# Two transformer-style layers on one core: the router's logits turned whole with the mean square as a column, two modulation chunks moved among the second layer's input projections, and the last output piece split at another point of ScalarE's order

## The chip, the cores and the metric

The kernel runs on one core of a Trainium2 chip. Time is the device time of one execution in microseconds (us). A core has TensorE (PE; PEld is its weight load), VectorE (DVE), ScalarE (ACT), GpSimd (POOL) and SyncE (SP), each with its own instruction stream, and 16 DMA engines that all queues share. Engines wait for one another by semaphores. TensorE's clock is granted at one of two levels, 1.2 or 2.4 GHz; the profile gives it as a share of 2.4.

## The reference, cut to what matters

Two layers over 128 context tokens and 512 latent tokens of width 1024, all in fp32. Each layer has mixers between an input and an output projection, then an expert-choice mixture of 16 experts (capacity 64 latent and 16 context tokens each). Six modulation vectors per layer and group come from a 1024 x 6144 product.

```python
for layer in range(DEPTH):
    sh1, sc1, g1, sh2, sc2, g2 = modulation(c, w_mod[layer], b_mod[layer])   # silu(c) @ w_mod + b_mod, in six
    h = rms_norm(x, norm1[layer]) * (1 + sc1) + sh1
    x = x + g1 * mixers(h)                       # input projections, attention and gating or conv, output projection
    h = rms_norm(x, norm2[layer]) * (1 + sc2) + sh2
    x = x + g2 * ec_moe(h, moe_router[layer], ...)
# ec_moe: aff = softmax(h @ w_router); gate, idx = top_k(aff, cap) for each expert; SwiGLU of the gathered rows
```

## The kernel before

**Layout.** The residual x is kept turned (`xT`: features on 128 partitions, 8 feature tiles of 640 tokens). A weight piece is 128 x 2048 elements (1 MB). It is loaded by SyncE into a place, split by ScalarE into a high part `w_hi` (`split`, L1582, L1593, L1886) and by VectorE into the rest `w_lo` (L1998, L1996), and multiplied by TensorE in three passes (`passes`, `project`, `project_by_rows`). There are four stage slots that go round in the order of the stream (`staged()` in `plan_weights`), some lent places in other buffers, and three split slots. A load waits for the last user of its slot: for a split piece until its low part is made (`lo_ready`), for a modulation half until TensorE has used it (`mod_used`, or the chunk's rows being full). SyncE issues the loads strictly in the order of the stream (L732), so a wait holds up all behind it.

**Modulation chunks.** 24 chunks of 512 columns (12 a layer), each two 1 MB halves that are not split. `mod_rows(c)` on TensorE makes the rows (16 matmuls on 32-column groups), ScalarE copies them from PSUM to `mrow`, `turn_mod(c)` turns them by four transposes, VectorE reduces and adds the bias (L2072, L2075). `MOD_AT` says where each chunk stands in the order; `mod_before` and `mod_place` follow from it. The two chunks of `"next norm"`, 16 and 17 (the gate of layer 1's mixers, used at its output projection), stand between layer 1's first norm and its first input projection `cq`.

**Orders written out by hand.** PSUM has 8 banks. `plan_psum` lists every use of a bank in TensorE's order and who empties it; `begin`, `filled` and `emptied` wait by that list. The four engine programs (`block.tensor`, `block.scalar`, `block.vector`, `block.gpsimd`) repeat the same order, each for its own part, so that an engine that waits holds up what stands behind it.

**Output projection (both layers).** Eight tiles m, two to a weight piece `(L, "out", j)`. VectorE adds each into x (L2322) and from m = 3 on makes `h_sum` = x times scale (L2340). Beneath the tiles TensorE does the chunks of `MOD_AT[(L, "out")]` (rows after an even m, turn after the next m). ScalarE splits piece 3, then goes through `squares_for_pool` (L1595): for each m it squares x (L1604), copies chunk rows (L1580), and after m = 0 the turned shift, which goes to DRAM. GpSimd adds the squares of tiles 0 to 6 (L812).

**Ranking.** The router's logits are made in four column groups of TensorE, each summing two feature tiles, as two halves of 320 tokens; squares summed over features come as one column per token tile (`token_sums`, weights = the squares, moving = one column of 1/1024). ScalarE copies the logits, TensorE turns them and adds the four groups at once by a product with `fold` (five token tiles, 16 columns each). VectorE and ScalarE make the root (L2344, L1625, L1628, L2347 to L2349), the softmax (L2358 to L2366). TensorE turns three row tiles of h, then the affinities (L1421), then two more row tiles, the rows of the chunks of `(L, "rank")` and, in layer 1, x. ScalarE scales and copies the row tiles, GpSimd adds the shift (L886), SyncE stores them (L780). VectorE picks the top 64 and 16 in rounds of eight (L2373 to L2376); after the second round it converts the context's indices (L2379, a cast) and adds 512 (L2380), at the end it converts the others (L2381). Then come the gates, the slots (L2393), the gathers (L895, which wait for all row stores and for the slots) and the experts.

**Start of layer 1.** When the experts' sum is read back (`acc_in`), TensorE turns it, VectorE adds it into x, ScalarE squares (L1684), TensorE sums, VectorE makes the variance (L2017), its part of the split of `cq`, and the root's Newton step. SyncE waits for `acc_in` before the first half of chunk 16. GpSimd waits for the second half of chunk 17 before its small loads. The input projections then run `cq`, `ckv`, `gc`, `hv`, `gb`, two pieces each of the last three.

## Time and profile before

| | |
|---|---|
| three timed runs | 1398.42 us median (1397.84 to 1402.41) |
| the profiled execution | 1397.08 us, span 1395.3 us, mean granted clock 0.947 |
| TensorE busy | 1272.9 us, 91% of the span |
| VectorE busy | 870.8 us, 62% |
| ScalarE busy | 707.4 us, 51% |
| GpSimd busy | 242.9 us, 17% |
| chain that ended last | TensorE 76%, DMA 10%, ScalarE 7%, VectorE 6% |

How to read it. The profile is of one execution; times in it are us from the start of the span. A line of the timeline gives start, length, engine, source line, operation, written and read tensors, shape and count, and in brackets how long the engine had been idle before it and what released it. TensorE's matmuls are pipelined and their ends are modelled; an fp32 matmul shows as two records. The layer-0 mixers run from 39 to 340 us, its ranking to 384, its experts to 674; layer 1 follows: input projections 711 to 831, attention to 964, output projections to 1034, ranking to 1076, experts to the end.

### The profile page before, as it was taken

The page shows a single profiled execution, that of the slowest core. Times are in us where ns is not written, and L with a number is a line of the kernel's source. Part 1 is how long each engine was busy: PE and PEld are TensorE (multiplying, and loading weights), DVE is VectorE, ACT ScalarE, POOL GpSimd, SP SyncE. Part 2 cuts the span into 40 slices and gives each one's busy share as a digit, 9 for nine tenths or more (in the row PEclk, how much of TensorE's full clock was granted, in tenths as well). Part 3 has the DMA queues.
Part 4 walks back from the last instruction along what each step waited for, and adds up shares of the span by engine and source line. Part 5 has one row for each costly group of instructions (what it writes and reads, how often), then busy time and mean ns, then how long its engine had stood idle before and what let it go on. Part 6 is the DMA issues. An engine that isn't in the chain of part 4 may idle for free.

```text
span 1395.3 us, 18223 instructions
## 1 busy us (share of the span) xinstructions
PE 1272.9 (91%) x7584; PEld 923.8 (66%) x7584; DVE 870.8 (62%) x1007; ACT 707.4 (51%) x821; POOL 242.9 (17%) x135
## 2 busy tenths in 40 slices
PE   5999988999399999999789998999994999999997
PEld 2887856788266666666469984667892666666562
DVE  5613556422678888888475252553226799999894
ACT  3531147511467777777343123554115677776772
POOL 3100000011502222211030000000124033333330
PEclk9997899999699999999989999899997999999997
DMA  9810182042799999999893221002409999999984
GB/s 358 248 63 31 39 290 82 1 151 91 285 350 350 385 380 380 384 392 396 289 267 103 91 82 57 1 1 91 151 31 356 372 381 378 385 387 382 398 295 160
DMA packets 100471, 324.98 MB, mean 233 GB/s; under 512 B 6719, under 2 KB 30494, under 8 KB 84006
## 3 DMA queue, kind: packets, MB, share of 16 engines
q1 hardware_dynamic: 89376, 290.88, 55.5%
q0 software_dynamic: 8400, 27.58, 7.8%
q10 hardware_dynamic: 2614, 5.35, 1.1%
q8 instruction: 60, 0.98, 0.3%
q14 instruction: 21, 0.17, 0.0%
HBM read 300.29 MB, written 23.50 MB: 232 GB/s over the span
## 4 chain that ended last, share of the span: by engine, by line
PE 76%; DMA 10%; ACT 7%; DVE 6%; issue 1%; SPq 0%; ACTq 0%
PE psum L939 71%; ACT arena L1812 3%; DMA stage<-in_w_mod 3%; DVE arena L2264 2%; DMA arena<-in_moe_w_up 2%; DMA h_hi<-h_dram,arena 2%; DVE w_lo L1996 1%; PE psum L1463 1%; DMA stage<-in_moe_w_gate 1%; ACT arena L1580 1%; DMA arena<-in_od_w_in 1%; ACT w_hi L1886 1%; PE psum L1412 1%; PE psum L1497 1%; PE psum L1016 1%
## 5 line engine op out<-in xcount | busy, mean ns | idle before, releaser
L939 PE MATMUL psum<-w_hi,h_hi 128*80 128x512 f32 (+1 forms) x848 | 330.6, 390 | 9.9 <-DVE w_lo L1996 6.5
L1996 DVE TENSOR_TENSOR w_lo<-stage,w_hi 128x2048 fp32r<-128x2048 f32 (+1 forms) x122 | 275.5, 2270 | 94.5 <-ACT w_hi L1593 56.4
L939 PE MATMUL psum<-w_lo,h_hi 128*80 128x512 f32 (+1 forms) x848 | 325.8, 384 | 0.0
L939 PE MATMUL psum<-w_hi,h_lo 128*80 128x512 f32 (+1 forms) x848 | 325.1, 383 | 0.0
L1886 ACT ACTIVATE w_hi<-stage 128x2048 fp32r<-128x2048 f32 x100 | 190.5, 1915 | 56.8 <-PE psum L939 37.0
L939 PE MATMUL psum<-h_hi,w_hi 128*128 128x320 f32 x672 | 214.3, 319 | 1.4 <-DVE h_lo L2043 1.4
L939 PE MATMUL psum<-h_hi,w_lo 128*128 128x320 f32 x672 | 211.5, 315 | 0.0
L939 PE MATMUL psum<-h_lo,w_hi 128*128 128x320 f32 x672 | 211.3, 315 | 0.0
L904 POOL DMA_INDIRECT acc_dram<-arena x31 | 120.2, 3879 | 411.0 <-ACT arena L1918 227.0
L1996 DVE TENSOR_TENSOR w_lo<-arena,w_hi 128x2048 fp32r<-128x2048 f32 x73 | 166.7, 2288 | 35.7 <-ACT w_hi L1886 31.8
L939 PEld LDWEIGHTS psum<-w_hi,h_hi 128*80 128x80 f32 (+1 forms) x848 | 129.9, 153 | 84.1 <-issue 14.0
L939 PEld LDWEIGHTS psum<-w_hi,h_lo 128*80 128x80 f32 (+1 forms) x848 | 129.9, 153 | 63.8 <-issue 1.6
L939 PE MATMUL psum<-arena 128*64 128x128 f32 (+7 forms) x964 | 147.3, 398 | 20.1 <-ACT arena L1812 9.9
L939 PEld LDWEIGHTS psum<-w_lo,h_hi 128*80 128x80 f32 (+1 forms) x848 | 130.2, 154 | 52.9 <-issue 1.2
L1886 ACT ACTIVATE w_hi<-arena 128x2048 fp32r<-128x2048 f32 x71 | 134.9, 1913 | 20.2 <-PE psum L939 16.1
L939 PEld LDWEIGHTS psum<-arena 128*64 128x64 f32 (+4 forms) x964 | 83.3, 177 | 86.9 <-issue 61.5
L939 PEld LDWEIGHTS psum<-h_hi,w_hi 128*128 128x128 f32 x672 | 129.9, 193 | 6.4 <-issue 6.2
L939 PEld LDWEIGHTS psum<-h_lo,w_hi 128*128 128x128 f32 x672 | 129.6, 193 | 0.2 <-issue 0.2
L939 PEld LDWEIGHTS psum<-h_hi,w_lo 128*128 128x128 f32 x672 | 129.3, 192 | 0.0
L1580 ACT ACTIVATE arena<-psum 128x512 f32<-128x512 f32 (+7 forms) x125 | 65.0, 576 | 99.3 <-PE psum L939 82.0
L1812 ACT ACTIVATE arena<-psum,arena 128x640 f32<-128x640 f32 x64 | 50.2, 789 | 63.5 <-DVE arena L2264 63.5
L2322 DVE SCALAR_TENSOR_TENSOR xT<-psum,mod,xT 128x320 f32<-128x320 f32 (+2 forms) x48 | 18.1, 433 | 100.0 <-PE psum L939 100.0
(267 smaller groups left out, 1315.1 us busy)
## 6 DMA issues: line engine op xcount, KB each, us to landing
stage<-in_w_mod SPq DMA_DIRECT2D x46, 1024.0 KB, 7.7
stage<-in_moe_w_up SPq DMA_DIRECT2D x36, 1024.0 KB, 15.7
stage<-in_moe_w_down SPq DMA_DIRECT2D x34, 1024.0 KB, 14.5
stage<-in_moe_w_gate SPq DMA_DIRECT2D x30, 1024.0 KB, 14.5
arena<-in_moe_w_gate SPq DMA_DIRECT2D x29, 1024.0 KB, 16.5
arena<-in_moe_w_up SPq DMA_DIRECT2D x23, 1024.0 KB, 15.2
arena<-in_moe_w_down SPq DMA_DIRECT2D x19, 1024.0 KB, 15.2
xT<-in_moe_w_down SPq DMA_DIRECT2D x11, 1024.0 KB, 20.6
```

Of the source, the lines that this page charges most:

```text
L904: pool.indirect_dma_start(acc_dram[L], bass.IndirectOffsetOnAxis(slots[:, e:e + 1], 0), ysb[e % 2], None, compute_op=ALU.add).then_inc(sca ...
L939: return pe.matmul(o, w, x, start=first, stop=last, skip_group_check=True)
L1016: ins = pe.transpose(bank(("mod turned", c))[:, P * b:P * b + P], mrow[:, P * b:P * b + P], ident)
L1412: ins = pe.transpose(pair((L, "h", t), n=D)[:, P * k:P * k + P], h_sum[k][:, P * t:P * t + P], ident)
L1463: ins = pe.transpose(psum[:, k // 4, CAP * (k % 4):CAP * (k % 4) + CAP], xs[s][:, P * k:P * k + P], ident[0:CAP, 0:CAP])
L1497: ins = pe.transpose(psum[:, 2, CAP * f:CAP * f + CAP], hid[:, P * f:P * f + P], ident[0:CAP, 0:CAP])
L1580: freeing(nc.scalar.activation(dst, src, ACT.Copy, **kw))
L1812: ins = nc.scalar.activation(p[:, LKEYS * a:LKEYS * a + LKEYS], src[:, 0:LKEYS], ACT.Exp, bias=largest(i, a), accum_out=total(i, a))
L1886: nc.scalar.activation(split_slot(w_hi, pc["q"]), slot(pc), ACT.Copy).then_inc(hi_ready, 1)
L1996: return nc.vector.tensor_tensor(dst, src, hi.bitcast(F32), ALU.subtract)
L2264: ins = nc.vector.tensor_reduce(largest(i, a), src[:, 0:LKEYS], AX.X, ALU.max, negate=True)
L2322: ins = nc.vector.scalar_tensor_tensor(xT[:, m, tk], src, mod[:, L, 2, m, g:g + 1], xT[:, m, tk], ALU.mult, ALU.add)
```

## The change

- Chunks 16 and 17 leave the start of layer 1. Chunk 16 stands after the second `gc` piece, chunk 17 after the second `hv` piece, in the weight stream and on all engines. SyncE waits for `acc_in` before `cq`, GpSimd for `cq`.
- The logits are made for 512 latent and 128 context tokens, in two banks. A matrix `mean_` (zeros, column 16 = 1/1024) is multiplied with the sum of squares in column group 0 and with the last square in group 1, so that row 16 of the groups holds the mean square. ScalarE copies the latent part, VectorE the context part, five transposes turn all, and VectorE adds the four groups by one reduction of 17 columns for five token tiles. The root is made from column 16, after the turn.
- Two row tiles, not three, are turned ahead of the affinities.
- ScalarE splits output piece 3 after the square of m = 1, inside `squares_for_pool`, instead of ahead of it.
- The two index conversions become one instruction each, max(index, index + 512) and max(index, index + 0), written as fp32.

```diff
-          "acc": [13, 14, 15], "next norm": [16, 17], "cq": [18, 19], ...
+          "acc": [13, 14, 15], "gc": [16], "hv": [17], "cq": [18, 19], ...
...
@@ plan_weights: the stream
-            chunk(MOD_AT["next norm"][0])
...
-            if kind == "cq":
-                chunk(MOD_AT["next norm"][1])
+            if (kind, m) in (("gc", 1), ("hv", 1)):
+                mod(kind)
...
@@ SyncE, GpSimd
-                    if L > 0 and pc["key"] == ("mod", MOD_AT["next norm"][0], 0):
+                    if L > 0 and pc["key"] == in_keys(L)[0]:
...
-                    pc = piece[("mod", MOD_AT["next norm"][1], 1)]
+                    pc = piece[in_keys(L)[0]]
...
@@ TensorE
-                    mod_rows(MOD_AT["next norm"][0])
-                    turn_mod(MOD_AT["next norm"][0])
-                    mod_rows(MOD_AT["next norm"][1])
...
-                    turn_mod(MOD_AT["next norm"][1])
...
                     project(("gc", 1), [("gc", 2), ("gc", 3)])
+                    modulation("gc")
                     for kind in ("hv", "gb"):
                         for j in range(2):
                             project((kind, j), [(kind, 2 * j), (kind, 2 * j + 1)])
+                        if kind == "hv":
+                            modulation("hv")
                     modulation("cq")
...
+                def column_group(g, weights, moving, tk, first, last):
+                    o = bank((L, "logits")) if tk is LAT else bank((L, "logits ctx"))[:, 0:NC]
+                    return mm(o[32 * g:32 * g + 32, :], weights, moving[:, tk], first, last)
+
+                for tiles in ((0, 1, 2, 3), (4, 5, 6)):
                     pe.wait_ge(x_scaled, KD * L + tiles[-1] + 1)
+                    for tk in GROUPS:
                         for k in tiles:
+                            column_group(k % 4, router[:, L, k, :], h_sum[k], tk, k < 4, k >= 4)
...
+                pe.wait_ge(mean_ones, 1)
                 pe.wait_ge(sq_added, added[0])
+                pe.wait_ge(x_scaled, KD * (L + 1))
                 pe.wait_ge(sq_ready, squared[0])
+                for tk in GROUPS:
+                    column_group(3, router[:, L, KD - 1, :], h_sum[KD - 1], tk, False, True)
+                    column_group(0, mean_[:, :], rstd, tk, False, True)
+                    column_group(1, mean_[:, :], sq[(KD - 1) % 2], tk, False, True).then_inc(psum_full, 1)
                 name = (L, "logits turned")
+                emptied(pe, (L, "logits ctx"))
+                emptied(pe, (L, "logits"))
                 begin(name)
                 for t in range(NT):
-                    at = E * TILE_AT[t]
-                    ins = mm(bank(name)[:, at:at + E], lgT[:, P * t:P * t + P], fold[:, :], t == 0, t == NT - 1)
+                    at = P * TILE_AT[t]
+                    ins = pe.transpose(pair(name)[:, at:at + P], lgT[:, P * t:P * t + P], ident)
...
-                for t in range(3):
+                for t in range(2):
                     turn_tile(t)
                 pe.wait_ge(aff_done, L + 1)
...
+                turn_tile(2)
                 turn_tile(3)
...
@@ ScalarE, squares_for_pool
                     if k % 2 == 0 and k // 2 < len(under):
                         modulation((L, "out"), slice(k // 2, k // 2 + 1))
+                    if which == 1 and k == 1:
+                        split((L, "out", 3))
...
@@ ScalarE, layer 1's projections
                     for m in (2, 3):
                         evacuate(("gc", m), two(zT[:, m, :]), halves(("gc", m)))
+                    modulation("gc")
                     split(keys[6])
                     split(keys[7])
                     split((L, "out", 0))
+                    modulation("hv")
                     split((L, "out", 1))
...
-                split((L, "out", 3))
                 squares_for_pool(L, 1, (L, "T", len(STEPS) - 1, 2))
-                evacuate((L, "logits"), two(lgT), halves((L, "logits")))
-                root_of(L, 1)
+                evacuate((L, "logits"), lgT[:, LAT], bank((L, "logits")))
+                act.wait_ge(token_var_ready, L + 1)
+                nc.scalar.activation(token_root, token_var, ACT.Ln).then_inc(log_done, 1)
...
@@ VectorE
+            then(nc.vector.memset(mean_[:, :], 0.0))
+            nc.vector.tensor_copy(mean_[:, E:E + 1], ones_d[:, 0:1]).then_inc(mean_ones, 1)
...
                     split(keys[5])
+                    modulation("gc")
                     split(keys[6])
...
                     split((L, "out", 0))
+                    modulation("hv")
...
+                freeing(nc.vector.tensor_copy(lgT[:, CTX], bank((L, "logits ctx"))[:, 0:NC]))
+                name = (L, "logits turned")
+                filled(dve, name)
+                parts = pair(name).rearrange("p (t g r) -> p t r g", t=NT, g=4)[:, :, 0:E + 1, :]
+                freeing(nc.vector.tensor_reduce(token_sums, parts, AX.X, ALU.add))
+                emptied(dve, name)
+                column = token_var.rearrange("p (t o) -> p t o", o=1)
+                nc.vector.tensor_scalar(column, token_sums[:, :, E:E + 1], EPS, None, ALU.add).then_inc(token_var_ready, 1)
...
-                        ctx_idx = idxf[CTX_ROW:RANKED, 0:CAP_C]
-                        then(nc.vector.tensor_copy(ctx_idx, idx[CTX_ROW:RANKED, 0:CAP_C]))
-                        nc.vector.tensor_scalar(ctx_idx, ctx_idx, float(NL), None, ALU.add).then_inc(ranked_ctx, 1)
-                nc.vector.tensor_copy(idxf[0:2 * E, :], idx[0:2 * E, :]).then_inc(topk_done, 1)
+                        found = idx[CTX_ROW:RANKED, 0:CAP_C]
+                        nc.vector.scalar_tensor_tensor(idxf[CTX_ROW:RANKED, 0:CAP_C], found, float(NL), found, ALU.add, ALU.max).then_inc(ranked_ctx, 1)
+                found = idx[0:2 * E, :]
+                nc.vector.scalar_tensor_tensor(idxf[0:2 * E, :], found, 0.0, found, ALU.add, ALU.max).then_inc(topk_done, 1)
```

## Rows read from the trace of the kernel before

**Rows 1.** The page: the span.
```profile
span 1395.3 us, 18223 instructions
```

**Rows 2.** The chain of waits (start, length, what it went through).
```profile
690.94 10.19 DMA arena<-in_od_w_in
...
741.76 89.20 PE psum L939 x598
```

**Rows 3.** The timeline of the output projections, layer 0 (first two) and layer 1.
```profile
290.49 0.42 PEld L1016 LDWEIGHTS psum<-cst,mrow 128*128 128x128 f32 x4 [3.64 <-ACT small L1580]
...
299.65 0.16 PEld L939 LDWEIGHTS psum<-stage,sP 128*32 128x32 f32 x8 [0.19 <-issue]
...
981.96 1.13 DVE L2322 SCALAR_TENSOR_TENSOR xT<-psum,mod,xT 128x320 f32<-128x320 f32 x3 [9.01 <-PE psum L939]
982.02 1.91 ACT L1593 ACTIVATE w_hi<-stage 128x2048 fp32r<-128x2048 f32 x1 [16.82 <-PE psum L939]
983.84 0.72 ACT L1604 ACTIVATE arena<-xT 128x640 f32<-128x640 f32 x1
...
985.30 0.71 PEld L1016 LDWEIGHTS psum<-cst,mrow 128*128 128x128 f32 x4 [3.64 <-ACT small L1580]
...
986.28 1.74 SPq L732 DMA_DIRECT2D stage<-in_w_mod  x3
...
995.53 1.92 PE L939 MATMUL psum<-stage,sP 128*32 128x512 f32 x16
```

**Rows 4.** Busy by stretch: us, PE, PEld, DVE, ACT, POOL, clock, DMA share, GB/s.
```profile
984.00:986.00 2.00, 0.67 (x3) 0.70 (x4) 2.00 (x1) 1.19 (x3) 0.00 (x0) 0.56 0.00 0
```

**Rows 5.** DMA issues, 291.4 to 291.7 us (count, size, us to landing).
```profile
stage<-in_w_mod SPq DMA_DIRECT2D x1, 1024.0 KB, 5.1
```

**Rows 6.** The timeline of the ranking, layer 0 (first two) and layer 1.
```profile
340.37 2.35 PE L939 MATMUL psum<-arena,router 128*32 128x320 f32 x28
...
353.26 0.38 PE L1421 MATMUL psum<-cst,arena 128*32 128x128 f32 x2
...
1034.10 2.35 PE L939 MATMUL psum<-arena,router 128*32 128x320 f32 x28
...
1037.59 1.26 PE L939 MATMUL psum<-arena,router 128*32 128x320 f32 x4
...
1040.17 0.17 DVE L2344 TENSOR_SCALAR stat<-psum 128x5 f32<-128x5 f32 x1 [3.87 <-PE psum L939]
...
1041.52 0.24 DVE L2358 TENSOR_TENSOR arena<-psum,stat 128x80 f32<-128x80 f32 x1
...
1043.41 0.24 DVE L2366 TENSOR_TENSOR arena<-arena 128x80 f32<-128x80 f32 x1
...
1045.03 0.64 PE L1421 MATMUL psum<-cst,arena 128*32 128x128 f32 x2
```

**Rows 7.** Groups of VectorE's instructions by shape (busy us, mean ns).
```profile
L2264 DVE TENSOR_REDUCE arena<-psum 128x1 f32<-128x640 f32 x64 | 49.7, 819 | 30.3 <-PE psum L939 30.3
```

**Rows 8.** The timeline behind the affinities, layer 0.
```profile
356.85 9.29 POOL L886 TENSOR_TENSOR arena<-arena,h_hi 128x1024 f32<-128x1024 f32 x4 [2.70 <-ACT arena L1580]
...
359.26 2.29 DVE L2380 TENSOR_SCALAR arena<-arena 16x16 f32<-16x16 f32 x1
...
372.37 0.80 SPq L774 DMA_DIRECT2D arena<-in_moe_w_gate  x2
```

**Rows 9.** The timeline at the start of layer 1.
```profile
693.12 2.77 ACT L1684 ACTIVATE arena<-xT 128x640 f32<-128x640 f32 x4 [0.95 <-DVE xT L2062]
...
698.96 0.82 DVE L2017 TENSOR_SCALAR arena<-psum 128x640 f32<-128x640 f32 x1 [1.44 <-PE psum L939]
...
701.15 1.91 ACT L1593 ACTIVATE w_hi<-arena 128x2048 fp32r<-128x2048 f32 x1 [5.25 <-DMA arena<-in_od_w_in]
...
703.09 2.29 DVE L1996 TENSOR_TENSOR w_lo<-arena,w_hi 128x2048 fp32r<-128x2048 f32 x1 [3.31 <-ACT w_hi L1593]
```

**Rows 10.** The timeline of the ranking in layer 1: the turn of a chunk.
```profile
1054.63 0.42 PEld L1016 LDWEIGHTS psum<-cst,mrow 128*128 128x128 f32 x4 [1.68 <-ACT mrow L1580]
```

More of the change, by code:

```diff
@@ L105 @@
 MOD_AT = {"start": [2, 3, 0, 1], "qk": [4, 5], "first scores": [6, 7], (0, "out"): [8, 9, 10], (0, "rank"): [11, 12],
-          "acc": [13, 14, 15], "next norm": [16, 17], "cq": [18, 19], (1, "out"): [20, 21], (1, "rank"): [22, 23]}
+          "acc": [13, 14, 15], "gc": [16], "hv": [17], "cq": [18, 19], (1, "out"): [20, 21], (1, "rank"): [22, 23]}
 def mod_before(c):
@@ L195, in plan_psum @@
             one((L, "norm", 0), "dve", 2)
-            chunk, later_chunk = MOD_AT["next norm"]
-            one(("mod rows", chunk), "act"), one(("mod turned", chunk), "dve", in_order=False), one(("mod rows", later_chunk), "act")
         if L == 0:
@@ L225, in plan_psum @@
             one(("cq", 0), "act", 2), one(("cq", 1), "act", 2)
-            one(("mod turned", later_chunk), "dve", in_order=False)
-            for c in MOD_AT["next norm"]:
-                p.frees(("mod turned", c))
             one("ckv", "act", 2), one("kr", "act", 2)
@@ L235, in plan_psum @@
             one(("gc", 2), "act", 2), one(("gc", 3), "act", 2)
-            for kind in ("hv", "gb"):
-                for m in range(4):
-                    one((kind, m), "dve", 2)
+            mod("gc")
+            for m in range(4):
+                one(("hv", m), "dve", 2)
+            mod("hv")
+            for m in range(4):
+                one(("gb", m), "dve", 2)
             mod("cq")
@@ L434, in trunk @@
         router_ = sb("router", LAYERS * KD * 32)
-        fold = sb("fold", E)
+        fold, mean_ = sb("fold", E), sb("mean", 32)
         cst = sb("cst", C_USED)
@@ L1376, in logits @@
                     pe.wait_ge(x_scaled, KD * L + tiles[-1] + 1)
-                    for half in range(2):
-                        tk = slice(HT * half, HT * half + HT)
+                    for tk in GROUPS:
                         for k in tiles:
-                            g = 32 * (k % 4)
-                            ins = mm(bank((L, "logits"), half)[g:g + 32, 0:HT], router[:, L, k, :], h_sum[k][:, tk], k < 4, k >= 4)
-                    return ins
-                def token_sums(squares, first):
-                    for t in range(NT):
-                        at = TILE_AT[t]
-                        ins = mm(bank((L, "norm", 1))[:, at:at + 1], squares[:, P * t:P * t + P], ones_d[:, 0:1], first and t == 0, not first)
-                    return ins
@@ L1413, in turn_tile @@
                     ins.then_inc(psum_full, 1)
-                for t in range(3):
+                for t in range(2):
                     turn_tile(t)
@@ L1619, in squares_for_pool, with root_of @@
                                  bank((L, "shift logits"))[:, 0:2].rearrange("p (g o) -> p g o", o=1).to_broadcast([P, 2, P]))
-            def root_of(L, which):
-                emptied(act, (L, "norm", which))
-                squared, root = (var, rstd) if which == 0 else (token_var, token_root)
-                nc.scalar.activation(root, squared, ACT.Ln).then_inc(log_done, 1)
+            def root_of(L):
+                emptied(act, (L, "norm", 0))
+                nc.scalar.activation(rstd, var, ACT.Ln).then_inc(log_done, 1)
                 logs[0] += 1
                 act.wait_ge(log_done, logs[0])
-                nc.scalar.activation(root, root, ACT.Exp, scale=-0.5).then_inc(root_done, 1)
+                nc.scalar.activation(rstd, rstd, ACT.Exp, scale=-0.5).then_inc(root_done, 1)
             def shifted(L):
@@ L1639, in shifted @@
                         modulation("start", slice(3, None))
-                    if L > 0 and k == 3:
-                        modulation("next norm", slice(1, 2))
             def modulation(at, part=slice(None)):
@@ L1673, in _ @@
             split(in_keys(0)[0])
-            root_of(0, 0)
+            root_of(0)
             modulation("start", slice(2, 3))
@@ L1678, in _ @@
                 if L > 0:
-                    filled(act, (L - 1, "norm", 1))
+                    filled(act, (L - 1, "logits ctx"))
                     for k in range(KD):
@@ L1686, in _ @@
                     split(keys[0])
-                    root_of(L, 0)
-                    modulation("next norm", slice(0, 1))
+                    root_of(L)
                 shifted(L)
@@ L2126, in _ @@
                 split(keys[1])
-                if L > 0:
-                    modulation("next norm")
                 split(keys[2])
```

40 lines of the change are left out of this document (17 added, 23 removed).

## The prediction, on record before the changed kernel was seen

> **What bounds the kernel now.** I read the page first. The profiled execution has a span of 1395.3 us [rows 1] and 1397.08 us in all, so 1.8 us lie around the span; the three timed runs have their median at 1398.42, 1.3 above it. Then the chain of waits: TensorE carries three quarters of it, with stretches such as 89.2 us of back-to-back projections in the second layer [rows 2]. So work moved onto TensorE inside such a stretch costs its whole length, and what matters elsewhere is each place at which TensorE waits. I went to four of them with the timeline: the output projections of both layers, the ranking between projections and experts, the start of layer 1, and the layer-1 projections into which the two chunks move.
>
> **Output projections (the split of output piece 3 moved on ScalarE).** The edit is small in the diff, but the timeline shows a stall there. At the end of output tile 1 ScalarE first splits piece 3 (982.02, 1.91 us), then squares x (0.72), and only then copies the chunk rows for which TensorE waits; TensorE idles 3.64 us and turns the chunk at 985.30 [rows 3]. Layer 0 has the same 3.64 us, ending at 290.49 [rows 3]. The granted clock falls with it, to a mean of 0.56 of 2.4 GHz, so it is at 1.2 GHz for most of that stretch [rows 4], and output tile 2, 48 matmuls that take 7.1 us at the pace of [rows 2] (89.2 / 598 = 0.149 each), takes 8.8 in layer 0 (to 299.65) and 9.5 in layer 1 (986.0 to 995.53) [rows 3]. With the change the square and the copies of tile 0 come first and TensorE turns its chunk at once. That would give back 5.1 and 5.8 us. But something is late next. The split of piece 3 now stands behind the update of x (1.13) and the square (0.72), so the low half is done about 1.8 us later, and its slot is what the second half of the next chunk is loaded into: SyncE issues that load at 986.28 now [rows 3], and would at 988.1. It lands 5.1 us later [rows 5], at 993.2, while TensorE wants it at 982.5 + 7.1 + 1.0 = 990.6. The chunk's rows (1.92 us, half behind the load) end at 994.1 in place of 997.4: a gain of 3.3. In layer 0 by the same sum the load is issued at 293.3, lands at 298.4, and the rows end at 299.4 in place of 301.6: 2.2. Each now has an idle of 2.8 us, somewhat shorter than the 3.64 after which the clock fell; if it falls again, 1.7 to 2.4 go. I take 0.8 off each: **-1.4 and -2.5**. Ends: -0.5 and -0.9; and -5.1 and -5.8 if nothing is late.
>
> **Ranking.** Both layers do the same from the first group of router matmuls, G (1034.10 and 340.37) [rows 6]. Now: 2.35 us of them, ten one-column matmuls, the last router tile (1.26), ten more, then the turn by the fold. The root starts at G + 6.07 (L2344), the affinities' first step at G + 7.42 (L2358); they are ready at 1043.65, but TensorE is in the third tile and turns them 1.4 us later, at G + 10.93; in layer 0, where the clock is low, at G + 12.89 [rows 6]. After: 2.35, then the last tile and the two sets of mean columns in three different column groups side by side, as the first 14 matmuls are now (2.35 for what would be 8.8 alone), so 1.26; a copy of 512 columns by ScalarE (0.6, as the 0.58 to 0.72 of its neighbours), five transposes (0.8), a reduction of 340 elements, which I put at 0.5 between the 0.24 of 80 elements [rows 6] and the 0.82 of 640 [rows 7], and an addition. That makes the root start at G + 5.5, L2358 at G + 6.8, the affinities ready at G + 8.95 and turned at G + 9.1, as only two tiles stand ahead. Gain 3.8 in layer 0 and 1.8 in layer 1.
>
> What it is worth is read behind it. GpSimd's shifts start after ScalarE's second row tile and run 9.29 us without a gap; the last store of the rows lands just before 372.37, when SyncE goes on to the next weights, and the gather waits for the same [rows 8]. All of that moves with the affinities. The merged index instructions take 4.1 us out of the ranking on VectorE (L2379 and L2380 wait for GpSimd's shifts; the second takes 2.29 for 16 columns [rows 8]). I cost them at nothing: the store's landing covers the chain, which is done at about the same time now and would be early by this. If the new form waits for one shift, that is at most 2.3 back, still beneath the stores. In layer 1 the gate turn also waits for ScalarE's copies of x, which move by the 1.8. Against the gain: the DMA engines are full from the first expert pieces on, and those go out when TensorE has used chunk rows that now stand behind the third tile, so they move by 1.4 less, 2.4 and 0.4. I take the middle, **-3.1 and -1.1**.
>
> Here SyncE's loads of weights and GpSimd's gathers meet. The Trainium skill (DMA: Bandwidth & Descriptors, section Queues, rings and completion order) says that each DMA engine takes turns between the queues that have work. By that rule the gather wouldn't wait out SyncE's backlog, and the term would be the full 3.8 and 1.8, the sum 1.4 lower. No row here shows the turns themselves.
>
> **Start of layer 1.** The first projection's weights are issued third, behind the two halves of the removed chunk, and land 10.19 us later, at 701.1; ScalarE splits them (701.15), VectorE forms the low half (703.09, 2.29), and only then come the root, the scaled tiles and the first matmul [rows 2, 9]. Put first, they land after 5.1 [rows 5], at 695.1. That two loads ahead cost 5.1 together shows that one queue serves them in order. ScalarE is then in its squares until 695.9 and splits by 697.9; VectorE is held by the norm (698.96, 0.82 [rows 9]) and makes the low half at 699.8 in place of 703.09. **-3.3**; 1.0 if the load should take 10.2 after all. The removed chunk work costs nothing there today (TensorE idle) and its removal gives nothing. GpSimd's small loads start earlier, which nobody waits for.
>
> **The two chunks.** Both go into the 89.2 us stretch, without cover. Chunk 16, after the second gc piece: rows 1.92, then TensorE waits for ScalarE's copy, as at 1054.63 where it turns the rows after 1.68 of idle on the weight side, 0.8 after their end, and 0.5 for the turn [rows 3, 10]: **+3.1**. Its loads and its ring neighbours are early.
>
> Chunk 17, after hv, has another wait. Stage slots go round in fours. In the new order the pieces behind the first one are ckv, gc0, gc1, 16a, 16b, hv0, hv1, 17a, 17b, gb0, gb1, out0: out0 has the slot of 17a. So SyncE can't issue out0 until TensorE has used 17a. ScalarE, in its order, splits out0 and only then copies the rows of chunk 17, and TensorE stands before the turn for that copy. From the start of the rows: 0.96 (first half), 5.1 for the load, 1.95 for the split, 0.65 for the copy, 0.6 for the turn: 9.3 us. The idle of 7 us in it is longer than the one that lowered the clock in [rows 3, 4], so I add 1.8 for the restart: **+11.1** (9.3 to 11.8). VectorE's conv work behind its own split of out0 fits under the gb tiles.
>
> Before, the turn of chunk 17 stood after cq in a gap. Sum: -1.4 - 2.5 - 3.1 - 1.1 - 3.3 + 3.1 + 11.1 = **+2.8**. Against the profiled execution 1397.08 + 2.8 = 1399.9; with the median's 1.3 above it, **1401.2 us**. With every own term at its ends the sum goes from -1.5 to +10, that is 1397 to 1408.
>
> **Rivals.**
> - A: the forecast, chance 0.50.
> - B, slower: the clock. After each of the three idles (two of 2.8 us, one of 7) TensorE stays at 1.2 GHz longer, as after 985.30, where tile 2 lost 2.4 us. It decides if the 2.8 us idles already lower it. Price 1.6 at each output stage, 1.5 more at chunk 17, and the ranking, which begins colder, gives 1 less: about +5.5, 1406.7. For it: the fall at 3.64 in both layers, and ranking at low clock in layer 0 only. Chance 0.22.
> - C, faster: the wait at chunk 17 isn't there, because the slots fall otherwise than I count or the load is issued earlier. The 11.1 becomes 3.1, the sum -5.2: 1393.2. For it: only that I counted a ring. Chance 0.10.
> - D, faster: the loads at the output stages are in time, and all of 5.1 and 5.8 comes back: -7.0 more, 1394.2. Against it is the moved split itself. Chance 0.10.
> - E: the change does almost nothing, 1398.4, because the gains at the ranking end in a full DMA queue and the chunks hide in something that I don't see. Chance 0.08.
>
> **How the numbers follow.** 0.3% is 4.2 us, about what a measurement of this kernel tells from no change: slower begins at 1402.6, faster ends at 1394.2. A lies with a third of its chance above 1402.6 (0.16), B wholly (0.22): slower 0.38. Faster: most of C and half of D, 0.14. The rest, 0.48, is within. The range 1395 to 1407 takes in A, B and E with half of D, and leaves out C and the upper end of A.
>
> **What would show it.** In the profile after: TensorE turns chunks 8 and 20 with no idle before it; an idle of about 3 us inside the rows of chunks 9 and 21, released by a load; the first matmul of layer 1 at about 3 us sooner after the norm; after hv one idle of about 7 us ahead of a turn, with a load of in_od_w_out and its split in it; the index instructions gone from 4.1 us to 0.3 to 2.4; the gather no earlier than the row stores. Wrong would be the forecast if the idle after hv is under 3 us, or if the clock stays low for over 5 us after one of the three idles.

## The result, and the profile after

| | median of the runs | ratio to the kernel before, 95% interval |
|---|---|---|
| first comparison, 8 runs each | 1403.30 us (before: 1395.17) | 1.0068 [1.0045, 1.0090] |
| the same kernel again (`after_again`), 12 runs against 35 | 1399.42 us (before: 1394.82) | 1.0034 [1.0012, 1.0057] |

The changed kernel is slower by 0.3 to 0.7%, some 5 to 9 us. Both intervals lie above 1, and they overlap. The forecast was +2.8 us, 1401.2. The kernel before, at 1398.42 in the three runs known then, has its median near 1395 in the longer series, so the forecast is measured by its difference.

The profiled execution of the changed kernel took 1398.48 us, the shortest of its eight. It hides part of the loss, so I read a second one beside it. The page's busy line after; TensorE was 91% busy before:

```profile
span 1396.3 us, 18165 instructions
...
PE 1262.2 (90%) x7550; PEld 913.4 (65%) x7550; DVE 868.8 (62%) x1011; ACT 708.1 (51%) x821; POOL 235.6 (17%) x135
```

The chain of waits gives the borders of the stages. First further rows of the kernel before, for comparison with [rows 2] (start, length, what):

```profile
268.44 11.42 PE psum L939 x104
...
373.11 10.81 DMA h_hi<-h_dram,arena
...
680.62 5.98 DMA arena<-acc_dram
...
836.72 19.86 PE psum L939 x68
...
962.22 2.36 PE psum L939 x40
...
1065.80 10.58 DMA h_hi<-h_dram,arena
```

The same of the changed kernel:

```profile
268.78 11.43 PE psum L938 x104
...
293.55 5.21 DMA stage<-in_w_mod
...
370.59 8.85 DMA h_hi<-h_dram,arena
...
677.79 6.23 DMA arena<-acc_dram
...
801.62 5.34 DMA stage<-in_od_w_out
...
846.31 19.86 PE psum L938 x68
...
970.45 11.43 PE psum L938 x104
...
1069.51 8.24 DMA h_hi<-h_dram,arena
```

A stage is the distance between two of these: output projections and ranking from the x104 (or x40) row to the landing of the gather, experts to the landing of `acc_dram`, and so on. `copy_first`, `split_after_shift` and `best` are experiments told below. Each column is one execution.

| stage, us | before | after | after_again | copy_first | split_after_shift | best | forecast of the change |
|---|---|---|---|---|---|---|---|
| up to output projections, layer 0 | 268.4 | 268.8 | 269.8 | 271.4 | 270.8 | 268.9 | 0 |
| output projections and ranking, layer 0 | 115.5 | 110.7 | 109.5 | 109.7 | 108.2 | 108.3 | -4.5 |
| experts, layer 0 | 302.7 | 304.6 | 303.7 | 303.9 | 302.7 | 302.5 | 0 |
| start of layer 1 and its projections | 150.1 | 162.3 | 162.4 | 153.2 | 154.0 | 150.6 | +10.9 |
| attention, layer 1 | 125.5 | 124.1 | 124.2 | 123.2 | 123.2 | 123.2 | 0 |
| output projections and ranking, layer 1 | 114.2 | 107.3 | 111.1 | 109.8 | 109.5 | 110.2 | -3.6 |
| the rest | 318.9 | 318.6 | 318.8 | 317.9 | 318.7 | 317.6 | 0 |

One row carries the loss: +12.2 and +12.3 us where the chunks went in. It stands against the gains of the two stages of outputs and ranking. In the first profile of after the second of these is -6.9, in the repeat -3.0; the three executions to the right lie between them, at -4.0 to -4.7. The timeline behind the `hv` piece, changed kernel, TensorE, ScalarE and SyncE:

```profile
800.49 1.92 PE L938 MATMUL psum<-stage,sP 128*32 128x512 f32 x16
809.43 1.11 PE L1015 MATMUL psum<-cst,mrow 128*128 128x128 f32 x4 [7.01 <-ACT mrow L1574]
...
806.98 1.91 ACT L1587 ACTIVATE w_hi<-stage 128x2048 fp32r<-128x2048 f32 x1 [18.49 <-DMA stage<-in_od_w_out]
808.80 0.58 ACT L1574 ACTIVATE mrow<-psum 128x512 f32<-128x512 f32 x1
...
801.62 1.23 SPq L731 DMA_DIRECT2D stage<-in_od_w_out  x2
```

TensorE uses the first half of chunk 17, SyncE can then issue output piece 0 (801.62), it lands after 5.34, ScalarE splits it (806.98) and only then copies the chunk's rows (808.80). TensorE idles 7.01 us for 0.58 us of copying.

### The profile page after: what moved, and what is told of

Same layout as the page of the kernel before. It is cut to its first block, busy times and chain, and to the rows that moved or that the text cites. A ratio compares the mean times of both kernels' runs of the same rounds, so it can differ in the third digit from the quotient of the medians.

```text
span 1396.3 us, 18165 instructions
## 1 busy us (share of the span) xinstructions
PE 1262.2 (90%) x7550; PEld 913.4 (65%) x7550; DVE 868.8 (62%) x1011; ACT 708.1 (51%) x821; POOL 235.6 (17%) x135
## 4 chain that ended last, share of the span: by engine, by line
PE 71%; DMA 9%; DVE 8%; ACT 8%; POOL 2%; issue 2%; ACTq 0%; POOLq 0%; DVEq 0%
PE psum L938 67%; ACT arena L1806 4%; DVE w_lo L1993 2%; DVE arena L2263 2%; DMA xT<-in_moe_w_up 2%; DMA arena<-in_moe_w_up 2%; POOL arena L885 1%; DMA stage<-in_moe_w_gate 1%; PE psum L1457 1%; DMA h_hi<-h_dram,arena 1%; DMA h_dram<-arena 1%; ACT w_hi L1883 1%; DMA stage<-in_w_mod 1%; POOL arena L811 1%; ACT arena L1574 1%
## 5 line engine op out<-in xcount | busy, mean ns | idle before, releaser
L903 POOL DMA_INDIRECT acc_dram<-arena x31 | 115.5, 3724 | 414.7 <-ACT arena L1915 228.5
L938 PEld LDWEIGHTS psum<-w_hi,h_hi 128*80 128x80 f32 (+1 forms) x848 | 129.8, 153 | 83.8 <-DVE w_lo L1993 13.7
L1598 ACT ACTIVATE arena<-xT 128x640 f32<-128x640 f32 x24 | 17.6, 738 | 118.2 <-DVE xT L2321 87.4
```

Of the source, the lines that this page charges most:

```text
L903: pool.indirect_dma_start(acc_dram[L], bass.IndirectOffsetOnAxis(slots[:, e:e + 1], 0), ysb[e % 2], None, compute_op=ALU.add).then_inc(sca ...
L938: return pe.matmul(o, w, x, start=first, stop=last, skip_group_check=True)
L1598: nc.scalar.activation(rstd if k == 0 else sq[k % 2], xT[:, k, :], ACT.Square).then_inc(sq_ready, 1)
```

## Which part costs, which gains

I took the change apart. The chunk move alone:

```diff
-          "acc": [13, 14, 15], "next norm": [16, 17], "cq": [18, 19], (1, "out"): [20, 21], (1, "rank"): [22, 23]}
+          "acc": [13, 14, 15], "gc": [16], "hv": [17], "cq": [18, 19], (1, "out"): [20, 21], (1, "rank"): [22, 23]}
```

and what follows from it on each engine; outputs and ranking as before.

> The kernel before with one part of the change alone: chunks 16 and 17 beneath the second layer's projections, cq weights loaded first; output stages and ranking as before. Theory (the forecast's terms -3.3 + 3.1 + 11.1): slower than before by about 11 us, ratio 1.008. Rival C (no wait at chunk 17): about 3 us slower, 1.002. If instead the whole change's +8 is mostly the ranking or the output stages, this run is within 3 us of before.

Measured: 1404.89 us, 1.0060 [1.0034, 1.0086], and the stage of the layer-1 projections takes 162.0, as in after. The whole is 8 to 10 us slower, near the theory's 11 and not rival C's 3; the attention behind is 2.3 shorter. The rest of the change, with the chunks back:

> The changed kernel with chunks 16 and 17 back ahead of the second layer's projections: the output-stage and ranking edits alone. Theory (terms -1.4 -2.5 -3.1 -1.1): 8 us faster than before, ratio 0.994. Rival (the gains at the output stages are eaten by the low clock, and those of the ranking by the DMA stream of the experts): within 3 us of before, ratio 0.998 to 1.002; then the 8 us by which the changed kernel is slower are nearly all the chunks'.

Measured: 1388.98 us, 0.9965 [0.9942, 0.9987]: the other edits are a gain, between the 0.994 of the theory and the 0.998 at which the rival began. And of them ScalarE's split alone:

```diff
-                split((L, "out", 3))
                 squares_for_pool(L, 1, (L, "T", len(STEPS) - 1, 2))
...
+                    if which == 1 and k == 1:
+                        split((L, "out", 3))
```

> The kernel before with ScalarE's split of output piece 3 moved behind the second square, nothing else. Forecast's terms: 3.9 us faster (0.9972), with an idle of 2.8 us in the rows of chunks 9 and 21. Rival B (TensorE falls to 1.2 GHz after that idle as well): 1 us faster at most, 0.999 to 1.000, and the clock in the stretch of output tile 3 near 0.5.

Measured: 1396.0 us, 1.0005 [0.9983, 1.0028]: nothing that this timing can see. Its profile has 114.0 for outputs and ranking of layer 0, -1.4 as forecast, and 114.4 for layer 1, where -2.5 was forecast. The idle that comes instead of the removed one is as forecast. In the changed kernel (timeline, TensorE in layers 0 and 1, then SyncE in layer 0):

```profile
298.80 1.72 PE L938 MATMUL psum<-stage,sP 128*32 128x512 f32 x8 [2.88 <-DMA stage<-in_w_mod]
...
1000.47 1.06 PE L938 MATMUL psum<-stage,sP 128*32 128x512 f32 x8 [2.86 <-DMA stage<-in_w_mod]
...
293.55 7.37 SPq L731 DMA_DIRECT2D stage<-in_w_mod  x5
```

The stage holds two things that were edited separately, so it has to be parted at the first router matmul. Before has it at 340.37 and 1034.10 [rows 6]; the changed kernel in layers 0 and 1, then `split_alone` in layer 1:

```profile
340.23 2.13 PE L938 MATMUL psum<-arena,router 128*32 128x512 f32 x22
...
1038.17 2.81 PE L938 MATMUL psum<-arena,router 128*32 128x512 f32 x29
```

```profile
1030.10 2.08 PE L939 MATMUL psum<-arena,router 128*32 128x320 f32 x25
```

| us | outputs, layer 0 | ranking, layer 0 | outputs, layer 1 | ranking, layer 1 |
|---|---|---|---|---|
| before | 71.9 | 43.6 | 71.9 | 42.3 |
| chunks_alone | 71.9 | 43.3 | 71.8 | 42.3 |
| split_alone | 71.3, clock fell | 42.7 | 70.4, clock fell | 44.0 |
| chunks_back | 69.8 | 40.1 | 69.0, clock fell | 42.0 |
| after | 71.5, clock fell | 39.2 | 67.7 | 39.6 |
| after_again | 70.0 | 39.5 | 67.5 | 43.6 |
| the eight later kernels | 68.2 to 71.4 | 39.6 to 41.4 | 66.0 to 70.4 | 41.9 to 44.2 |
| forecast of the change | -1.4 | -3.1 | -2.5 | -1.1 |

So the split of piece 3 does gain in both layers. Behind the new idle the clock fell in some executions and held in others: where it fell the gain is 0.5 to 0.6 us in layer 0 and 1.5 to 2.9 in layer 1, where it held 2.0 to 2.1 and 4.1 to 4.4. In `split_alone` it fell in both layers (stretch, us, TensorE busy, clock, DMA share, GB/s):

```profile
298.50:300.50 2.00, 1.97 (x9) 0.50 1.05 392
990.90:992.90 2.00, 2.00 (x10) 0.60 1.05 393
```

That is rival B in both layers of this kernel; in the changed kernel's first profile it fell in layer 0 only, in the second in neither. In layer 1 `split_alone` then loses 1.7 us in the ranking, which it didn't touch: the same part of it, 6 to 10 us behind the first router matmul, ran at a lower clock than before. `split_alone`, then before:

```profile
1036.00:1040.00 4.00, 4.00 (x20) 0.50 0.00 0
```

```profile
1040.00:1044.00 4.00, 4.00 (x31) 0.78 0.00 0
```

The ranking's edits gain 2 to 4 us in layer 0, in all eleven profiles that have them. In layer 1 they gain nothing that lasts: the eleven have 42.5 us in the mean, before has 42.3. The rows of h are ready 2.2 us sooner there (GpSimd's shifts end at 1060.03, 21.9 us behind the first router matmul, before at 24.1), but the gather comes 9.5 to 13.7 us behind the shifts, when the last row store has landed. In before it comes 7.6 behind them, and the trace names VectorE as what it waited for last (the slots are done at 1064.94). Before, then `after_again`, GpSimd:

```profile
1065.80 2.92 POOL L895 DMA_INDIRECT h_hi<-h_dram,arena  x1 [7.61 <-DVE mod L2072]
```

```profile
1071.76 0.98 POOL L894 DMA_INDIRECT h_hi<-h_dram,arena  x1 [12.48 <-DMA h_dram<-arena]
```

So the gain of the change is for the most part the ranking in layer 0 and the split in layer 1. Which of the ranking's edits gives it isn't separated, apart from the index instructions below. The parts alone add to 1.0025, the whole again:

> The changed kernel once more, unaltered. The parts measured alone add to +2 to +4 us (two chunks +8.4, ranking and split -4.9), the whole was timed at +9.4. If the parts add up, this run gives 1.002 to 1.004 of before; if there is an interaction of the parts, 1.006 to 1.008 again.

Measured 1.0034 [1.0012, 1.0057]: they add up within the intervals, and no interaction is shown.

## The wait at chunk 17

```diff
+                    modulation("hv")
                     split((L, "out", 0))
-                    modulation("hv")
                     split((L, "out", 1))
```

> The changed kernel, but ScalarE copies the rows of chunk 17 before it splits output piece 0. Theory (TensorE's wait after hv is the load of output piece 0 and its split, queued ahead of the copy): the idle shrinks from about 7 us to about 1, the stretch of projections by 6 to 8 us, and the whole is 6 to 9 us faster than the changed kernel, within 2 us of the kernel before (ratio 0.998 to 1.002). Rival (the wait is for the second half of chunk 17 or for VectorE): no change, ratio 1.006.

Measured: 1394.23 us, 0.9991 [0.9967, 1.0014], 5 us below the changed kernel's 1399.42 and 9 below its 1403.3; the stage falls by 9.1 us, 162.3 to 153.2. The theory held, with an idle of 0.78 and a little more than its 6 to 8 us in the stage. TensorE's turn:

```profile
803.62 0.66 PE L1015 MATMUL psum<-cst,mrow 128*128 128x128 f32 x4 [0.78 <-ACT mrow L1574]
```

The load of output piece 0 and its split are still there (issued at 802.04, split at 807.35) and cost nothing, since nobody stands behind them. The stretch after it, the same 192 matmuls, takes 28.17 us in place of 30.00: 1.8 us were the clock. The changed kernel, then `copy_first`, as stretches:

```profile
810.00:820.00 10.00, 10.00 (x57) 0.78 0.76 278
```

```profile
810.00:820.00 10.00, 10.00 (x70) 1.00 0.79 290
```

## Start of layer 1: is it the order of the loads?

The change loads the `cq` weights first. Can one have that and keep both chunks' rows in TensorE's idle time? From chunks_back:

```diff
-            chunk(MOD_AT["next norm"][0])
...
             if kind == "cq":
+                chunk(MOD_AT["next norm"][0])
                 chunk(MOD_AT["next norm"][1])
```

> As chunks_back (both chunks ahead of the second layer's projections), but the weights of the first projection are loaded ahead of chunk 16 and 17. Theory: the earlier weights alone are what the change gains at the start of layer 1 (forecast -3.3), and the chunks' rows still fit in TensorE's idle before the first projection: 3 us faster than chunks_back, ratio 0.994. Rival (the chunks' rows now arrive after the first scaled tile is ready and hold TensorE): within 1 us of chunks_back or slower, with an idle at the rows of chunk 17.

Measured: 1393.63 us, 0.9999 [0.9973, 1.0025]. The rival held: the stage takes 149.0 us, against 149.2 in chunks_back. Timeline and chain:

```profile
704.89 1.94 PE L941 MATMUL psum<-stage,sP 128*32 128x512 f32 x8 [2.98 <-DMA stage<-in_w_mod]
708.74 1.93 PE L941 MATMUL psum<-stage,sP 128*32 128x512 f32 x8 [1.91 <-DMA stage<-in_w_mod]
...
689.76 18.93 DMA stage<-in_w_mod
```

The second half of chunk 17 is the fifth megabyte behind the same start and lands at 708.7. Here both chunks' rows stand ahead of the first projection, so it waits for all five loads; in chunks_back it waits for the weights instead, and from the read-back to its start they take 23.5 and 23.6 us. (This kernel's whole time is also above that of chunks_back, 1388.98; the intervals overlap. In the profiles its experts of layer 0 take 308.2 us against 303.5, of which 3.8 are a read-back of 9.98 us in place of 6.18, and the rest behind layer 1's ranking 318.7 against 313.3; neither was edited.) So one chunk alone in the gap, and the other after `hv` with its copy first:

```diff
-          "acc": [13, 14, 15], "gc": [16], "hv": [17], "cq": [18, 19], (1, "out"): [20, 21], (1, "rank"): [22, 23]}
+          "acc": [13, 14, 15], "next norm": [16], "hv": [17], "cq": [18, 19], (1, "out"): [20, 21], (1, "rank"): [22, 23]}
...
+            if kind == "cq":
+                mod("next norm")
```

> As copy_first, but chunk 16 stands in TensorE's idle time ahead of the second layer's first projection, loaded behind the cq weights; chunk 17 stays after hv. Theory (what held TensorE in cq_first was the fifth load, chunk 17's second half, 18.9 us after its issue; chunk 16's came in time): chunk 16 costs nothing there, and the first layer-1 matmul comes as early as in copy_first; 3.1 us faster than copy_first. Rival (ckv weights, two loads later, hold the second group): an idle of over 1 us ahead of ckv and a gain under 1.

Measured: 1390.70 us, 0.9970 [0.9948, 0.9992], 3.5 below copy_first by the medians, with overlapping intervals; what shows the gain is the stage, 150.2 against 153.2, forecast -3.1. The rest of its profile, the longest of its twelve runs, is worse: the clock fell behind both late loads at the output projections, and outputs and ranking take 112.8 and 113.4 us against 109.7 and 109.8. Chunk 16's rows wait 2.61 us for their load and still end before the first scaled tile is there:

```profile
702.05 1.07 PE L942 MATMUL psum<-stage,sP 128*32 128x512 f32 x8 [2.61 <-DMA stage<-in_w_mod]
703.89 1.11 PE L1019 MATMUL psum<-cst,mrow 128*128 128x128 f32 x4 [0.78 <-ACT mrow L1578]
707.25 0.61 PE L942 MATMUL psum<-h_hi,w_hi 128*128 128x320 f32 x1 [2.25 <-DVE h_lo L2044]
```

Two chunks in the gap still give the shortest stage, 149.2 and 149.0 us; moving one out of it never paid there. It does save 0.84 us later. In the five profiles with both chunks in the gap TensorE waits for a copy by ScalarE in the attention, in the nine others it doesn't. Before:

```profile
863.05 0.94 PE L939 MATMUL psum<-arena 64*128 64x128 f32 x12 [0.84 <-ACT arena L1580]
```

## The late load at the output projections

First attempt: on top of copy_first, the split of piece 3 in tile 0, right behind the copy of the chunk's rows, and VectorE's half after the update of tile 0.

> As copy_first (chunk 17's rows copied before the split of output piece 0), and output piece 3 is split by ScalarE and VectorE during output tile 1, after the copy of the first chunk's rows, while both engines wait for TensorE. Theory: the load of the second half of chunk 9 / 21 is issued about 6 us sooner than in copy_first's profile, TensorE's idle in those rows falls from about 3 us to under 1.8, and the clock holds: 3 to 6 us faster than copy_first, ratio to before 0.995 to 0.997. Rival (the piece's place in the split ring isn't free so early, or the queue is full): within 2 us of copy_first.

Measured: 1391.06 us, 0.9979 [0.9951, 1.0006], 3.2 below copy_first by the medians, which is between theory and rival. TensorE no longer idles over 1 us for the late load, but the rival's reason was right and my reason for the edit was wrong: the ring place isn't free until TensorE has ended output tile 1, and the copy of the shift, whose bank the turn of chunk 8 needs, now stands behind that wait; TensorE idles 2.31 us for it. ScalarE and TensorE in layer 1:

```profile
980.41 1.91 ACT L1587 ACTIVATE w_hi<-stage 128x2048 fp32r<-128x2048 f32 x1 [6.62 <-PE psum L938]
982.23 0.25 ACT L1574 ACTIVATE small<-psum 16x128 f32<-16x128 f32 x1
...
982.63 0.67 PE L1015 MATMUL psum<-cst,mrow 128*128 128x128 f32 x4 [2.31 <-ACT small L1574]
```

Second attempt, behind the shift's copy and ahead of the next square:

```diff
-                    if which == 1 and k == 1:
-                        split((L, "out", 3))
...
+                        split((L, "out", 3))
...
-                    if m == 1:
+                    if m == 0:
                         split((L, "out", 3))
```

> As copy_first, with output piece 3 split by ScalarE after the shift's copy in tile 0 and before the square of tile 1 (in split_tile0 the same split stood ahead of the shift's copy, whose bank the turn of chunk 8 needs, and TensorE idled 2.3 us for it). Theory: the split starts when TensorE ends output tile 1, chunk 8 is turned at once, the load of the second half of chunk 9 is issued 2.3 us sooner than in copy_first, and the idle in its rows falls from 2.9 to about 1; each output stage gains 2 us or a little more with the clock held: 4 us faster than copy_first. Rival (the split still blocks something on the way to the turn): an idle of over 2 us ahead of the turn of chunk 8 and no gain.

Measured: 1386.74 us, 0.9956 [0.9934, 0.9977], 7.5 below copy_first by the medians, 4.9 by the ratios, with overlapping intervals. The outputs up to the first router matmul show 3.5 of it (68.2 and 66.0 us against 69.9 and 67.8), in executions in which the clock held in both kernels; in layer 1 the ranking gives 1.5 of that back (43.5 against 42.0). No idle at the turn; in the rows 1.17 and 1.15 in place of 2.9:

```profile
299.12 1.07 PE L938 MATMUL psum<-stage,sP 128*32 128x512 f32 x8 [1.17 <-DMA stage<-in_w_mod]
...
987.19 1.07 PE L938 MATMUL psum<-stage,sP 128*32 128x512 f32 x8 [1.15 <-DMA stage<-in_w_mod]
```

The same split on the chunks_back side:

> cq_first with output piece 3 split during output tile 1, as in split_tile0. If both theories hold, the two gains add to those of the ranking: about 10 us faster than before, ratio 0.991 to 0.994, the fastest of all. Rival: no better than chunks_back, 0.9965.

This one has the first attempt's place for the split. Measured 1389.38 us, 0.9967 [0.9944, 0.9990]: the rival's number, as both of its theories had fallen. And the two edits that held by their stages, together:

> one_in_gap and split_after_shift together, on top of copy_first. If both theories hold, 7 us faster than copy_first, about 8 to 10 faster than the kernel before: ratio 0.993. Rival: both gains are eaten by the DMA stream of the experts, ratio 0.997.

Measured: 1383.08 us, 0.9932 [0.9910, 0.9955]. It is faster than the kernel before by 12 us by the medians, 9.5 by the ratio, and some 16 to 20 faster than the changed one. Its layer-1 projections take 150.6 us, as before, with one chunk beneath them. It keeps the gain of the ranking in layer 0 (40.2 us), not in layer 1 (44.2), and the outputs take 68.2 and 66.0. Both chunks in the gap together with this split, that is chunks_back with the second attempt, wasn't run; by the stages above (149 + 125.5 us against 150.6 + 123.2 for projections and attention) my estimate is about the same time.

## The index instructions

The forecast costed the merged conversions at nothing. The old ones put back into copy_first, the context's two instructions and the copy for the others:

```diff
-                        nc.vector.scalar_tensor_tensor(idxf[CTX_ROW:RANKED, 0:CAP_C], found, float(NL), found, ALU.add, ALU.max).then_inc(ranked_ctx, 1)
...
-                nc.vector.scalar_tensor_tensor(idxf[0:2 * E, :], found, 0.0, found, ALU.add, ALU.max).then_inc(topk_done, 1)
...
+                        then(nc.vector.tensor_copy(ctx_idx, idx[CTX_ROW:RANKED, 0:CAP_C]))
+                        nc.vector.tensor_scalar(ctx_idx, ctx_idx, float(NL), None, ALU.add).then_inc(ranked_ctx, 1)
+                nc.vector.tensor_copy(idxf[0:2 * E, :], idx[0:2 * E, :]).then_inc(topk_done, 1)
```

> As copy_first, with the two-instruction conversion of the context's indices back. Theory (the forecast's zero): VectorE's chain ends 2 us later and is still done before the stores of the rows land; the gather is issued right after the store as in copy_first, and the time is that of copy_first within its interval. Rival: the gather waits for VectorE, and both rankings become 1 to 2 us longer, ratio 0.002 above copy_first.

Measured: 1392.52 us, 0.9985 [0.9964, 1.0006], no different from copy_first's 0.9991; the two stages of outputs and ranking are 109.5 and 109.6 us against 109.7 and 109.8. VectorE and GpSimd of this kernel:

```profile
352.67 1.89 DVE L2383 CAST arena<-arena 16x16 f32<-16x16 uint32 x1
354.60 2.30 DVE L2384 TENSOR_SCALAR arena<-arena 16x16 f32<-16x16 f32 x1
...
367.15 0.16 DVE L2396 TENSOR_TENSOR arena<-arena,psum 64x16 f32<-64x16 f32 x1
...
352.16 9.33 POOL L885 TENSOR_TENSOR arena<-arena,h_hi 128x1024 f32<-128x1024 f32 x4 [0.92 <-ACT arena L1574]
370.05 1.27 POOL L894 DMA_INDIRECT h_hi<-h_dram,arena  x1 [8.56 <-DMA h_dram<-arena]
```

Even with both conversions the chain on VectorE is done near 367, and the gather is issued at 370.05, when the row stores have landed. With one instruction the chain ends earlier and the gather doesn't.

## Why the prediction was right, and by how much it was off

- **Sign and place.** The cost is the chunk move, the gains are at outputs and ranking, and the sum is a small loss. The stage terms of after_again add to -6.0 + 1.0 + 12.3 - 1.3 - 3.0 = +3.0 us, beside a start that was 1.3 later; forecast +2.8. By the medians the loss is +4.6 in the second comparison and +8.1 in the first, which is close to rival B's +8.3. Behind the idles of 2.9 us the two profiles show B's low clock in one of four places only, but the profile of the first comparison is its shortest run, with a mean clock of 0.948, and the other seven have 0.942 to 0.945. So how much of B there was in them stays open.
- **Chunk 17** was forecast at 9.3 + 1.8 = 11.1. From the start of its rows to the first matmul of the next projection are 9.7 us (800.49 to 810.20), with 1.8 of clock behind: 11.5. Its terms held one by one: load 5.34 (5.1), split 1.91 (1.95), copy 0.58 (0.65); the turn ran at the low clock, 1.11 for 0.66. Rival C, no wait, is out: without the wait (`copy_first`) the stage is 9.1 shorter.
- **Chunk 16**: from its rows at 769.05 to the next projection at 772.16 are 3.1 us; forecast 3.1.
- **Start of layer 1**: from the read-back of the sum to the first projection, 24.5 before (686.60 to 711.12), 21.6 after (684.02 to 705.58): -3.0, forecast -3.3. With this the stage is +12.2, forecast +10.9.
- **Output stages.** The late load was issued at 293.55 (forecast 293.3) and the idle was 2.88 (2.8). Rival D, loads in time, is out. The forecast's -1.4 and -2.5 are a middle that no execution has: -0.5 and -2.0 in layer 0, -4.2 and -4.4 in layer 1, by whether the clock fell. The 0.8 that the forecast took off each is an average of two outcomes. In layer 1 it had the late load issued 1.8 us later than in before; it was 0.7 (24.8 against 24.1 us behind the start of the stage), and the 1.1 is missing from the forecast. That `split_alone` shows exactly -1.4 in layer 0 is luck: -0.6 at the outputs and -0.8 in a ranking that it didn't edit.
- **Ranking.** Forecast -3.1 and -1.1; measured -4.3 and -4.0 in layer 0, -2.7 and +1.3 in layer 1. The affinities are turned 8.9 us after the first router matmul (1038.17 to 1047.06 in layer 1), forecast 9.1, before 10.93 [rows 6]. That step held; what it is worth in layer 1 didn't: the last row store lands 8.6 us after its issue in the first profile of after, 11.6 in the second, 12.8 in best, and over eleven executions the gain is gone. That is rival E's reason, for one of the two layers; why the store takes that long isn't shown. The Trainium skill's rule (DMA: Bandwidth & Descriptors, section Queues, rings and completion order) gave the full 3.8 and 1.8. Over eleven executions layer 0 has 3.6 in the mean, between the two, and layer 1 nothing, below both; no row shows the engines' turns, so this doesn't decide it.
- **Attention.** I costed nothing here, and it is 1.3 shorter: 0.84 is the wait at 863.05 that is gone, the rest isn't explained.
- **Experts.** I costed nothing here; the layer-0 stage is 1.9 and 1.0 us longer after. It is 302.7 in before and in split_after_shift, where the ranking is the same as after's, and 304.0 in chunks_alone, where it is before's. Where these 1 to 2 us come from is open.

I gave 0.48 to a change within 0.3% and 0.38 to slower by more; both series lie beyond 0.3%, the second only just. The mechanism was right at the largest term, 11.5 of a forecast 11.1. That the sum of the profiles comes out at the forecast is in part luck: the first profile's ranking in layer 1 (39.6) is the shortest of eleven, and the misses at outputs, ranking, attention and experts cancel. The 1401.2 is near the first comparison's 1403.30 because the kernel before came out 3.2 us lower there than in the three runs known then. The low end of the sum, -1.5, doesn't come out of its terms either: with the full 2.2 and 3.3 at the outputs they add to -2.0, with rival D's 5.1 and 5.8 to -7.4.

## What to carry to other kernels

When work is moved under a long stretch of matmuls, follow the ring of buffers one turn round: here 0.6 us of copying waited behind the split of a piece that couldn't even be loaded until the chunk had been used. Putting the short copy ahead of the split costs no instruction and gave back 9 us of the stage. Before work is moved out of an idle gap, count how many loads fit in it ahead of the work behind: one chunk's did, two chunks' did not, and changing only their order gained nothing. And part a stage where two edits meet: one sum for outputs and ranking hid that the gain came from different edits in the two layers.

## What the runs showed of the hardware that was not expected

- **An idle under 3 us lowers TensorE's clock sometimes.** An idle of 2.7 to 2.9 us stands in both output stages of eight profiles (after, after_again, copy_first, chunks_back, split_alone, cq_first, one_in_gap, index_two_steps). The granted clock fell behind six of these sixteen (0.83 in the stretch 294 to 304 of after, layer 0) and stayed at 1.00 behind the other ten, in the same kernel at that:

```profile
294.00:304.00 10.00, 7.12 (x41) 4.54 (x40) 1.14 (x3) 1.33 (x2) 1.52 (x1) 0.83 0.96 342
...
1002.00:1012.00 10.00, 10.00 (x72) 10.00 (x71) 3.09 (x9) 0.99 (x2) 1.15 (x1) 1.00 0.89 327
```

  Behind 1.1 to 1.2 us (split_after_shift and best, four places) it never fell, behind 2.31 (split_tile0 and cq_first_split0) in two of four, behind 3.4 between matmuls (before and chunks_alone) in four of four. Behind the 7 us it fell in the two profiles of after and in chunks_alone (192 matmuls in 30.00, 30.09 and 29.50 us). Where it fell behind the 2.9, the outputs took 1.2 to 2.9 us longer than where it held.
- **The scatter between executions goes mostly with this clock.** The kernel before took 1385.07 us at a mean granted clock of 0.955 and 1402.60 at 0.942, in one series of 35; over the series 0.01 of clock goes with about 12 us, and in every other series here time falls as the clock rises too. So a single profile has to be read beside its clock, and small gains by stage and not by the whole time.
- **VectorE behind GpSimd.** The merged index instruction, 16 by 16 elements, takes 1.89 us at 353.23 in the changed kernel; it ends at 355.12, where GpSimd's first shift of 2.33 us (9.33 for four) ends that began at 352.72. The form for 32 by 64 elements takes 0.21 when GpSimd has finished:

```profile
353.23 1.89 DVE L2383 SCALAR_TENSOR_TENSOR arena<-arena 16x16 f32<-16x16 uint32 x1
...
352.72 9.33 POOL L885 TENSOR_TENSOR arena<-arena,h_hi 128x1024 f32<-128x1024 f32 x4 [0.92 <-ACT arena L1574]
...
363.52 0.21 DVE L2385 SCALAR_TENSOR_TENSOR arena<-arena 32x64 f32<-32x64 uint32 x1
```

  That agrees with the Trainium skill (SBUF — State Buffer, section Who interferes with whom): a VectorE instruction with two inputs in SBUF contends with a GpSimd instruction that reads SBUF. The two old conversions have one such input each, which this sentence doesn't cover; in index_two_steps they take 1.89 and 2.30 us and end at 354.56 and 356.90, where GpSimd's first two shifts end.
